# Half-slab weight pieces, paired transposes and an earlier slot marking in a mixture-of-experts loop

## The reference

```
logits = h @ w_router + b_router;  top 4 of 32 experts, gates = softmax(top 4)
for each expert e, for its tokens:
    gu = x_tok @ w_gu[e] + b_gu[e]               # 1024 x 2048
    gate, up = min(gate, 7), clip(up, -7, 7)
    h = (up + 1) * gate * sigmoid(1.702 * gate)
    y = h @ w_down[e] + b_down[e]                # 1024 x 1024
    out[token] += y * gate weight
```

## Time and profile before

| | us |
|---|---|
| median of 3 runs | 2474.75 (2472.07 to 2478.4) |
| the profiled execution's own time | 2473.07 |
| its span, first to last instruction | 2471.3 |
| PE busy in the span | 2281.1 |
| DVE busy | 1771.8 |
| ACT busy | 1412.0 |
| PE's granted clock, mean | 0.963 of full |

### The profile page before, as it was taken

How to read it: one execution, slowest core, us unless ns; L and a number is a source line. 1 busy time by engine, 2 the same in 40 slices (tenths; PEclk the granted TensorE clock), 3 DMA queues, 4 the chain that set the end, 5 groups by cost and what they waited for, 6 DMA issues and landing times.

```text
span 2471.3 us, 37393 instructions
## 1 busy us (share of the span) xinstructions
PE 2281.1 (92%) x10580; PEld 1677.8 (68%) x10581; DVE 1771.8 (72%) x3318; ACT 1412.0 (57%) x2108; POOL 286.6 (12%) x224
## 2 busy tenths in 40 slices
PE   8999998789997599999999999999999999999992
PEld 3544448468654288877777877878787787787872
DVE  0486785446335567787987889787978978878797
ACT  0368624555221255576766667565757757656575
POOL 0001931100010001110011011010101101111010
PEclk9999998799998599999999999999999999999996
DMA  4100002000204366786997889786978978868794
GB/s 170 69 5 34 1 17 103 0 1 1 94 1 151 148 202 221 226 299 227 357 320 237 282 288 341 272 290 216 354 255 294 358 248 300 296 223 290 233 311 183
DMA packets 80493, 489.28 MB, mean 198 GB/s; under 512 B 12147, under 2 KB 13427, under 8 KB 29331
## 3 DMA queue, kind: packets, MB, share of 16 engines
q1 hardware_dynamic: 67024, 450.06, 50.7%
q0 software_dynamic: 11440, 34.10, 6.2%
q10 hardware_dynamic: 1974, 4.43, 0.5%
HBM read 462.32 MB, written 33.69 MB: 201 GB/s over the span
## 4 chain that ended last, share of the span: by engine, by line
PE 70%; DVE 15%; issue 7%; ACT 3%; DVEq 2%; DMA 1%; ACTq 0%; POOL 0%; POOLq 0%; SPq 0%
PE ps L812 8%; PE ps L810 8%; PE ps L811 8%; DVE wlo L1627 8%; PE ps L538 6%; PE ps L807 6%; PE ps L808 6%; PE ps L549 5%; PE ps L730 5%; PE ps L831 4%; PE ps L712 2%; DVEq L382 2%; PE ps L693 1%; PE ps L700 1%; PE ps L579 1%
## 5 line engine op out<-in xcount | busy, mean ns | idle before, releaser
L1627 DVE TENSOR_TENSOR wlo<-raw,whi 128x1024 fp32r<-128x1024 f32 x776 | 931.0, 1220 | 189.2 <-ACT whi L1103 147.8
L1103 ACT ACTIVATE whi<-raw 128x1024 fp32r<-128x1024 f32 x776 | 817.7, 1060 | 375.8 <-PE ps L812 346.7
L811 PE MATMUL ps<-wlo,xhi 128*128 128x512 f32 x1024 | 400.2, 391 | 0.0
L812 PE MATMUL ps<-whi,xlo 128*128 128x512 f32 x1024 | 400.1, 391 | 0.0
L810 PE MATMUL ps<-whi,xhi 128*128 128x512 f32 x1024 | 400.1, 391 | 0.0
L812 PEld LDWEIGHTS ps<-whi,xlo 128*128 128x128 f32 x1024 | 193.0, 188 | 40.7
L811 PEld LDWEIGHTS ps<-wlo,xhi 128*128 128x128 f32 x1024 | 193.0, 188 | 40.4
L810 PEld LDWEIGHTS ps<-whi,xhi 128*128 128x128 f32 x1024 | 193.0, 188 | 38.5
L810 PE MATMUL ps<-whi,hhi 128*128 128x512 f32 x512 | 210.1, 410 | 0.0
L812 PE MATMUL ps<-whi,hlo 128*128 128x512 f32 x512 | 201.2, 393 | 0.0
L811 PE MATMUL ps<-wlo,hhi 128*128 128x512 f32 x512 | 200.2, 391 | 0.0
(11 more groups left out here) (343 smaller groups left out, 3349.4 us busy)
## 6 DMA issues: line engine op xcount, KB each, us to landing
raw<-in_w_gu SPq DMA_DIRECT2D x260, 1024.0 KB, 5.3
raw<-in_w_dn SPq DMA_DIRECT2D x128, 1024.0 KB, 5.1
raw<-in_w_out SPq DMA_DIRECT2D x2, 2048.0 KB, 13.6
h1all<-in_x SPq DMA_DIRECT2D x4, 1024.0 KB, 8.4
hext<-h1all SPq DMA_DIRECT2D x8, 512.0 KB, 12.0
acc<-accst SPq DMA_DIRECT2D x8, 512.0 KB, 2.6
fin<-acc SPq DMA_DIRECT2D x4, 1024.0 KB, 8.3
out<-fin SPq DMA_DIRECT2D x8, 512.0 KB, 2.6
```

Of the source, the lines that this page charges most:

```text
L811: pe.matmul(bank_ap, hi, wlo[:, slot, col, :], start=False, stop=False)
L812: return pe.matmul(bank_ap, lo, whi[:, slot, col, :], start=False, stop=stop)
L1103: act.activation(whi[:, j % 2, 2 * g:2 * g + 2, :], raw[:, (j + 2) % 3, 2 * g:2 * g + 2, :], ACT.Copy)\
L1627: dve.tensor_tensor(wlo[:, j % 2, s, :], raw[:, (j + 2) % 3, s, :], whi[:, j % 2, s, :].bitcast(f32), ALU.subtract).then_inc(lo_done, 1)
```

## The change

Five edits:

1. **Half-slab pieces.** `take_hi`, `take_lo` and every wait on hi_done, lo_done and piece_used go from four pieces of 128 x 1024 to two of 128 x 2048 in each slab. The transfers stay as they are.
2. **Transposes in longer runs.** h0 moves behind gate_up(2), directly ahead of h1. x0 and x1 follow each other behind down row 4, x2 and x3 behind row 6. `turned_hi` and `turned_lo` of h0 and h1 are both done at j = 2, behind the last piece of that turn.
3. **Two-column index.** cb has two columns for each tile, token within the tile and 128 t - 4096. find_index copies two results and makes one sum, 4096 added.
4. **Early marks.** mark_slots moves from the end of DVE's item to the place behind `turned_lo` of x1.
5. **The end of an item.** The second half of slab 7 moves behind ysb on ACT (which gets a wait for piece_used of the whole item ahead of ysb) and behind tail_out on DVE.

```diff
 # PE, item
                 gate_up(1, i, n1, blocks)
+                gate_up(2, i, n1, blocks)
                 turn_h(0, i, n1, blocks)
-                gate_up(2, i, n1, blocks)
                 turn_h(1, i, n1, blocks)
...
-                down(range(2, 3), i, n1, blocks)
+                down(range(2, 4), i, n1, blocks)
+                pe.wait_ge(tr_free[0], fill_of(i, "h", 2))
+                down(range(4, 5), i, n1, blocks)
 
                 pe.wait_ge(tokens_in, i + 2)
                 turn(xg, (1, 0), 0, fill_of(i, "x", 0))
-                down(range(3, 4), i, n1, blocks)
                 turn(xg, (1, 0), 1, fill_of(i, "x", 1))
-                down(range(4, 5), i, n1, blocks)
+                down(range(5, 7), i, n1, blocks)
                 turn(xg, (1, 0), 2, fill_of(i, "x", 2))
-                down(range(5, 6), i, n1, blocks)
                 turn(xg, (1, 0), 3, fill_of(i, "x", 3))
-                down(range(6, 8), i, n1, blocks)
+                down(range(7, 8), i, n1, blocks)
 # ACT
-                    act.activation(whi[:, j % 2, 2 * g:2 * g + 2, :], raw[:, (j + 2) % 3, 2 * g:2 * g + 2, :], ACT.Copy)\
+                    act.activation(whi[:, j % 2, 4 * g:4 * g + 4, :], raw[:, (j + 2) % 3, 4 * g:4 * g + 4, :], ACT.Copy)\
...
-                    take_hi(j + 2, (3,), i)
-                    if j:
-                        turned_hi(hhi, j - 1, fill_of(i, "h", j - 1), blocks)
-                take_hi(6, (0, 1), i)
+                    take_hi(j + 2, (1,), i)
+                    for quarter in ((), (), (0, 1), (2,))[j]:
+                        turned_hi(hhi, quarter, fill_of(i, "h", quarter), blocks)
+                take_hi(6, (0,), i)
                 biases(ex)
                 turned_hi(hhi, 3, fill_of(i, "h", 3), blocks)
-                take_hi(6, (2,), i)
+                take_hi(6, (1,), i)
                 turned_hi(xhi, 0, fill_of(i, "x", 0))
-                take_hi(6, (3,), i)
                 turned_hi(xhi, 1, fill_of(i, "x", 1))
                 take_hi(7, (0,), i)
                 turned_hi(xhi, 2, fill_of(i, "x", 2))
-                take_hi(7, (1,), i)
                 turned_hi(xhi, 3, fill_of(i, "x", 3))
-                take_hi(7, (2, 3), i)
...
+                act.wait_ge(piece_used, i * 12 + 12)
                 for n in range(2):
                     act.activation(ysb[:, 0, n * SLAB:(n + 1) * SLAB], ps[Y_BANK[0][n]][:, :], ACT.Copy,
                                    scale=gcol[:, 0:1]).then_inc(y_done[0], 1)
+                take_hi(7, (1,), i)
 # DVE
-                dve.scalar_tensor_tensor(out=slot_a[:, 0, :], in0=slot_n[:, :, 1], scalar=float(P), in1=slot_n[:, :, 0],
-                                         op0=ALU.mult, op1=ALU.add).then_inc(idx_step, 1)
-                dve.tensor_scalar(slot_a[:, 1, :], slot_n[:, :, 2], -4096.0, 4096.0, ALU.mult, ALU.add).then_inc(idx_step, 1)
-                dve.wait_ge(idx_step, steps)
                 dve.wait_ge(idx_kept, kept)
-                dve.tensor_tensor(idx_next[:, :], slot_a[:, 0, :], slot_a[:, 1, :], ALU.add).then_inc(idx_done, 1)
+                dve.scalar_tensor_tensor(out=idx_next[:, :], in0=slot_n[:, :, 0], scalar=float(NOWHERE), in1=slot_n[:, :, 1],
+                                         op0=ALU.add, op1=ALU.add).then_inc(idx_done, 1)
...
-                take_lo(6, (0, 1), i)
+                take_lo(6, (0,), i)
                 turned_lo(hhi, hlo, 3, fill_of(i, "h", 3, 0), blocks)
-                take_lo(6, (2,), i)
+                take_lo(6, (1,), i)
                 turned_lo(xhi, xlo, 0, fill_of(i, "x", 0, 0))
-                take_lo(6, (3,), i)
                 turned_lo(xhi, xlo, 1, fill_of(i, "x", 1, 0))
+                mark_slots(ex, i + 2, i + 3)
                 take_lo(7, (0,), i)
                 turned_lo(xhi, xlo, 2, fill_of(i, "x", 2, 0))
-                take_lo(7, (1,), i)
                 turned_lo(xhi, xlo, 3, fill_of(i, "x", 3, 0))
-                take_lo(7, (2, 3), i)
                 if len(blocks) == 2:
                     tail_out(n1)
-                mark_slots(ex, i + 2, i + 3)
+                take_lo(7, (1,), i)
```

More of the change, by code:

```diff
@@ L491, in load_slab @@
                     last = (j + 3) % 6
-                    piece_split(sp, i, last, 2 * part + 1)
+                    piece_split(sp, i, last, part)
                     sp.dma_start(raw[:, (j + 2) % 3, ks, :], src[:, ks, :]).then_inc(s[(j + 2) % 3], 16)
@@ L820, in find_slots @@
                     for t in range(NT):
-                        ins = pe.matmul(ps[TR_BANK[0]][:, 4 * b:4 * b + 3], slots[:, t, b * P:(b + 1) * P],
-                                        cb[:, 2 * P + 3 * t:2 * P + 3 * t + 3], start=t == 0, stop=t == NT - 1)
+                        ins = pe.matmul(ps[TR_BANK[0]][:, 4 * b:4 * b + 2], slots[:, t, b * P:(b + 1) * P],
+                                        cb[:, 2 * P + 2 * t:2 * P + 2 * t + 2], start=t == 0, stop=t == NT - 1)
                 ins.then_inc(tr_full[0], 1)
@@ L859, in down @@
                     for k in ks:
-                        if b == blocks[0]:
-                            piece_split(pe, i, j, k % 4)
+                        if k % 2 == 0 and b == blocks[0]:
+                            piece_split(pe, i, j, k % 4 // 2)
                         for n in range(2):
@@ L864, in down @@
                                           k == 0, k == KT - 1)
-                        if b == 0:
+                        if b == 0 and k % 2:
                             ins.then_inc(piece_used, 1)
@@ L1114, in gated @@
             def gated(quarter, i, n1, blocks):
-                act.wait_ge(piece_used, i * 24 + (4 * quarter + 4))
+                act.wait_ge(piece_used, i * 12 + (2 * quarter + 2))
                 n, uses = gu_place(0, quarter, i, n1, blocks)
@@ L1180, in _ @@
                 act.wait_ge(out_of[b], len([1 for v in PLACE.values() if v[0] == b]))
-            take_hi(0, range(4))
-            take_hi(1, range(4))
+            take_hi(0, range(2))
+            take_hi(1, range(2))
             for pair in range(4):
@@ L1694, in item @@
                                           None, ALU.mult).then_inc(gate_cp, 1)
-                        find_index(fills_before(i, 0) + 1, i * 2 + 4, i + 1)
-                    else:
-                        turned_lo(hhi, hlo, j - 1, fill_of(i, "h", j - 1, 0), blocks)
-                take_lo(6, (0, 1), i)
+                        find_index(fills_before(i, 0) + 1, i + 1)
+                    for quarter in ((), (), (0, 1), (2,))[j]:
+                        turned_lo(hhi, hlo, quarter, fill_of(i, "h", quarter, 0), blocks)
+                take_lo(6, (0,), i)
                 turned_lo(hhi, hlo, 3, fill_of(i, "h", 3, 0), blocks)
-                take_lo(6, (2,), i)
+                take_lo(6, (1,), i)
                 turned_lo(xhi, xlo, 0, fill_of(i, "x", 0, 0))
-                take_lo(6, (3,), i)
                 turned_lo(xhi, xlo, 1, fill_of(i, "x", 1, 0))
+                mark_slots(ex, i + 2, i + 3)
                 take_lo(7, (0,), i)
                 turned_lo(xhi, xlo, 2, fill_of(i, "x", 2, 0))
-                take_lo(7, (1,), i)
                 turned_lo(xhi, xlo, 3, fill_of(i, "x", 3, 0))
-                take_lo(7, (2, 3), i)
                 if len(blocks) == 2:
                     tail_out(n1)
-                mark_slots(ex, i + 2, i + 3)
+                take_lo(7, (1,), i)
             starts(dve, gu_read)
@@ L1730, in _ @@
             dve.memset(hb[TAIL:P, 1, :], 0.0).then_inc(tail_const, 1)
-            find_index(1, 2, 0)
-            take_lo(0, range(4))
-            take_lo(1, range(4))
+            find_index(1, 0)
+            take_lo(0, range(2))
+            take_lo(1, range(2))
             mark_slots(entry(0, 1, NE - 1), 1, 2)
@@ L1900, in constants @@
     c[:, C_ONE:C_ONE + P] = 1.0
-    b = np.zeros((P, 2 * P + 24), np.float32)
+    b = np.zeros((P, 2 * P + 2 * NT), np.float32)
     b[:, 0:P] = 1.0
```

50 lines of the change are left out of this document (24 added, 26 removed).

## The result

| | before | after |
|---|---|---|
| median of six runs, us | 2476.35 (2472.07 to 2478.4) | 2432.2 (2427.42 to 2433.92) |
| the profiled execution's own time | 2473.07 | 2429.33 |
| its span | 2471.3 | 2427.5 |
| PE busy | 2281.1 | 2275.2 |
| DVE busy | 1771.8 | 1716.3 |

The ratio is 0.982, with a 95% interval of 0.9807 to 0.9833. The two profiled executions differ by 43.7 us; the forecast had 53.4.

What follows compares the result with a forecast made beforehand. DVE was taken to bound one-block items. Savings of 41.0, 15.3, 0.6 and 1.0 us less 4.5 summed to 53.4, so 2419.7 for the profiled execution and 2421.5 us for the median; range 2404 to 2450.

Steps and rivals of the forecast that it cites:

- DVE sets the pace of a one-block item, and its loop head is part of that: One-block items: DVE busy 36.53 us plus a 2.26 us loop-head hole make 38.8 of 39.3.
- Half pieces save 0.08 us of fixed cost each time: DVE's pieces: 2.20 us for a half against 2.28 for two quarters, twelve times, 1.0 us saved an item.
- The price in latency: Longer pieces through PE, ACT and DVE: new PE waits of 0.1 us at h2, 0.35 at h3, 0.25 at x1.
- Longer runs save 0.05 us: PE's transposes: merging three pairs of runs saves 0.05 us an item, bounds 0 and 3 x 0.09.
- Marks: DVE's marks: still 2.0 us, but find_slots no longer waits; items behind tail and one-block items take the same 37.6 us.
- PE's floor is 36.75: One-block item if PE never waited: products, find_slots, refill and transposes sum to about 36.8 us.
- part 2: The forecast's part on longer transpose runs on PE: 0.05 us saved an item, with h0 off the late index copy.
- 37.6: Forecast length in us of a one-block item, from 39.3 - 1.0 - 0.3 - 0.45 = 37.55 on DVE.
- A term of the other sign: Tail item's gate_up(0): 0.5 us of new wait for x2 in each of 9 tail items, -4.5 us.
- Loop body at T + 7.4: DVE's last piece starts at T + 3.4 and its loop body 4.0 us later, with 1.8 us of hole showing.
- rival b: Transfers become the bound near 347 GB/s; with pieces or loop head saving nothing, 2435 to 2457 us, chance 0.22.

Runs made afterwards that it cites:

- e8: Kernel before with only the marks moved early, behind x1's turn; 2451.01 us, ratio 0.9901.
- e12: Kernel before, still with quarter pieces, with early marks and two of DVE's four table reads moved out of its loop head; 2434.74 us, ratio 0.9834.
- e2: Changed kernel with two of DVE's four table reads moved from its loop head to where their values are used; 2426.0 us, ratio 0.9804.
- e5: Changed kernel with half-slab pieces undone, each again two quarters in direct succession; 2447.0 us, ratio 0.9889.
- e4: Changed kernel with the transposes put back in their old places and shorter runs; 2475.9 us, ratio 1.0003.
- e11: Kernel before with only half-slab pieces and two-column index, x0 and x2 taken out one half piece sooner; 2524.92 us, ratio 1.0202.
- e6: Changed kernel with the marks back at the end of DVE's item, behind the last piece; 2475.15 us, ratio 0.9995.
- e1: Changed kernel with one more table read, its value unused, at the head of PE's loop; 2449.52 us, ratio 0.9893.
- e3: Changed kernel with two DVE table reads moved late and PE's x2 and x3 moved behind down row 5; 2433.26 us, ratio 0.9832.
- e9: As e7, against the changed kernel, with x2 and x3 also taken out ahead of slab 7's first half on ACT and DVE; 2409.0 us, ratio 0.9729.
- e7: As e3, against the changed kernel, with x0 and x1 taken out ahead of slab 6's second half on ACT and DVE; 2424.4 us, ratio 0.9791.

## Why the prediction was right, and where its size was off

The direction, the place and the range held; the gain was 43.7 us where 53.4 were forecast. Step by step:

- **DVE sets the pace of a one-block item, and its loop head is part of that**: shown for the kernel before by e8 and e12. With the head under two pieces a one-block item behind another fell from 39.3 to 37.7 us, with two reads out of the head to 37.0. In the changed kernel it holds by a little only: e2 took DVE's hole away and gained 0.3.
- **Half pieces save 0.08 us of fixed cost each time**: the piece is 2.288 us long and blocks for 2.20, so 1.0 us an item; e5 took 0.7 to 1.2 back. "VectorE: DVE Perf Modes" of the Trainium skill, errata section, gives 2291 ns for 2048 numbers; the measured 2288 agrees with it. Mine from the slope was 2270.
- **The price in latency**: waits of 0.1 at h2, 0.35 at h3 and 0.25 at x1 were laid out; in the item shown the list gives 0.3 at h3 and 0.3 in the x0, x1 run (1.07 us against 0.79 for the free one). Right. That this price is so small only with the new places of the turns, the forecast did not say; e4 and e11 show it.
- **Longer runs save 0.05 us**: by the rows they save 0.02 at most, one of eight costs as much as two of four. The value lies in the places (e4: 44 us). The forecast named h0 for that and gave it no price of its own.
- **Marks**: items behind a tail item and others became equal, 38.3 and 38.3, as forecast. e6 and e8 put the place of the marks at 43 us in the new order and 25 in the old.
- **The step that missed by most: "PE's floor is 36.75"**, with everything else in PE's way at DVE. It left out that PE has a loop head as well. In the kernel before, rows 6 and 7, 2.8 us, followed PE's last wait and covered it; in the new order only row 7 does, 1.4 us, and part 2 had no line for that. PE is idle there for 0.5 us in each of 18 items, and since products in a stream start every 0.23 us though each lasts 0.39, the loss is 0.16 more, some 0.7. That it is the head, e1 (one read more, longer wait), e3 (covered, gone) and the sequencer's records show. But it isn't simply the 0.7 us by which one-block items missed 37.6, 13 us in 19 of them. With DVE out of the way (e2) they took 38.0: e9's 37.07, some 0.8 of head, 0.2 of wait for x0. So 0.4 of the 0.7 is PE's path, whose floor the forecast also had 0.3 too low; the other 0.3 is waits for DVE, which e2 gave back. That head and miss come to the same number is chance.
- **A term of the other sign**: the 0.5 us that tail items were to wait for x2, 4.5 us in all, did not come, tail items stayed at 60.6. PE reached its first product later, by its loop head, and x2 was out at T + 1.7 and not at 2.6 (T is the start of gate_up(0)). e7 and e9, where the head is covered, show the wait coming and going with DVE's order. So 13 us too much gain and 4.5 too little nearly make up the 9.7 by which the forecast was off.
- **"Loop body at T + 7.4" held, behind one-block items by luck.** Behind the tail item shown, the last piece starts at T + 3.3 and the body at T + 7.3, each as laid out. Behind the one-block item the piece starts at T + 2.4, 1.0 sooner than forecast, since ACT had ysb at T - 0.7 while PE still was in its head; the longer reads gave 0.7 of it back, T + 7.1. Why two of the four reads are longer there is open.
- **Transfers** (rival b) were no bound: no wait of ACT names one, and e9 moved 360 and 362 GB/s over whole one-block items. "DMA: Bandwidth & Descriptors" of the Trainium skill, specifications, has 358 GB/s as a core's share of the memory; an estimate from it would put an item of 13.6 MB at 38.0 or more. It took 37.07, so the measurement decides against it here. The stated range ended at 2450, though (b) by its own numbers went to 2457.

Undone one at a time, edits 2, 4, 5 and 1 cost 44, 43, 28 and 15 us, three times the gain in sum: each needs the others, and no share of the 44 us belongs to one alone. The runs don't say what edit 3, the index, does; it was never undone by itself.

## What to carry to other kernels

In a rolled loop every engine has a head. Here it started, on PE and on DVE, only when the engine's last wait of the turn was over: count the work that follows that wait on each engine, not only on the slow one, before moving a waiting instruction toward the end. Price an edit of grain (longer pieces) together with the places of the waits that it must meet: in the old order it cost 2%, with the turns and marks moved it gave 15 us. When two paths lie within 1 us of each other, a fix of one gives the difference and no more; e9 paid only when all three waits of PE went. And try the smallest move first: e12, two moves on DVE, was as fast as the five edits.

## What the runs showed that was not expected

- One more table read on PE is 0.8 us of wait of its weight loads in each item; it costs 0.5 us of a one-block item's time and 0.7 of a tail item's.
- The eight marks took 1.72 us in the kernel before and 1.53 in the changed one. It is not DVE's loop head beside them: in e6 the head runs beside them too, and they took 1.53. The cause is open.
- POOL's copy of two numbers, 442 ns in the kernel before (mean of 30), took 1178 ns in the changed one, with the same operands. The mean mixes three cases: 0.19 us in tail items, and 1.38 or 2.08 in one-block items. The long ones lie beside a piece on DVE and end 0.04 us behind it, all 19 of them:

```profile
L1844 POOL COPY idx_cur<-idx_mid 128x2 uint32<-128x2 uint32 x30 | 35.3, 1178 | 0.2
```

```profile
1069.94 2.29 DVE L1623 TENSOR_TENSOR wlo<-raw,whi 128x2048 fp32r<-128x2048 f32 x1
1070.89 1.38 POOL L1844 COPY idx_cur<-idx_mid 128x2 uint32<-128x2 uint32 x1
```

So here a copy on POOL that starts while DVE subtracts two tiles is done only when DVE is, and a longer piece holds it longer: in the kernel before, with pieces of 1.22 us, the longest was 1.06. Only POOL's own next copy waited for it, which cost nothing here.
